# Retention outputs of the first key tile in three single passes, with weights and values split into a rounded part and a remainder

## The reference, cut to what matters

```python
scores = jnp.einsum('bhncd,bhnsd->bhncs', qf, kf) * decay[None, :, None]
o_intra = jnp.einsum('bhncs,bhnse->bhnce', scores, vf)
```

## Time and profile before

| | |
|---|---|
| median of 3 runs | 1299.32 us (1299.04 to 1299.36) |
| the profiled execution | 1299.08 us, its span 1297.3 us |
| PE busy | 1275.5 us, 98% |
| DVE busy | 881.3 us, 68% |
| ACT busy | 684.4 us, 53% |
| POOL busy | 49.4 us, 4% |
| chain that ended last | PE 97%, DVE 1%, ACT 1% |
| mean granted TensorE clock | 0.997 |

### The profile page before, as it was taken

The page is one execution under the profiler, slowest core; times in us unless marked ns, Lnnn a source line. Parts: engine busy times, 40 slices in busy tenths (PEclk is TensorE's granted clock), DMA queues, the critical chain, the costliest instruction groups (busy, mean ns, idle before and its releaser), DMA issues.

```text
span 1297.3 us, 26115 instructions
## 1 busy us (share of the span) xinstructions
PE 1275.5 (98%) x10282; PEld 1270.3 (98%) x10282; DVE 881.3 (68%) x1098; ACT 684.4 (53%) x894; POOL 49.4 (4%) x47
## 2 busy tenths in 40 slices
PE   6999999999999999999999999999999999999996
PEld 6999999999999999999999999999999999999996
DVE  7666555877775786665566665568788777766654
ACT  5444445757766554444454444457578565544531
POOL 1000001000000010000010000010000001000000
PEclk9999999999999999999999999999999999999998
DMA  7555555544334555555545555545543444655551
GB/s 273 190 171 175 177 172 172 178 163 147 131 129 134 174 168 179 179 176 178 179 163 182 175 178 178 178 165 179 172 137 131 147 160 165 208 183 193 172 193 59
DMA packets 61217, 219.30 MB, mean 169 GB/s; under 512 B 6992, under 2 KB 8144, under 8 KB 61008
## 3 DMA queue, kind: packets, MB, share of 16 engines
q1 hardware_dynamic: 60704, 217.53, 50.3%
q10 hardware_dynamic: 432, 0.59, 0.1%
HBM read 217.04 MB, written 1.05 MB: 168 GB/s over the span
## 4 chain that ended last, share of the span: by engine, by line
PE 97%; DVE 1%; ACT 1%; DMA 0%; issue 0%; DVEq 0%; ACTq 0%
PE bank L984 31%; PE bank L983 31%; PE bank L985 31%; PE bank L1105 1%; PE bank L1196 1%; PE bank L1225 1%; PE bank L1094 1%; DVE w_lo L611 0%; PE bank L1077 0%; DMA gain<-gains 0%; DVE xg L619 0%; PE bank L1112 0%; PE bank L997 0%; PE bank L1237 0%; PE bank L1095 0%; ACT xh L396 0%
## 5 line engine op out<-in xcount | busy, mean ns | idle before, releaser
L611 DVE TENSOR_TENSOR w_lo<-raw,w_hi 128x1024 fp32r<-128x1024 f32 x408 | 511.1, 1259 | 258.5 <-ACT w_hi L390 252.6
L983 PE MATMUL bank<-xh,w_hi 128*128 128x272 f32 (+1 forms) x2240 | 644.1, 288 | 11.9 <-DVE xl L625 11.4
L984 PE MATMUL bank<-xl,w_hi 128*128 128x272 f32 (+1 forms) x2240 | 642.2, 287 | 0.0
L985 PE MATMUL bank<-xh,w_lo 128*128 128x272 f32 (+1 forms) x2240 | 640.3, 286 | 0.0
L390 ACT ACTIVATE w_hi<-raw 128x1024 fp32r<-128x1024 f32 x408 | 428.7, 1057 | 398.4 <-PE bank L985 393.2
L983 PEld LDWEIGHTS bank<-xh,w_hi 128*128 128x128 f32 x2240 | 423.3, 189 | 12.9 <-DVE xl L625 10.3
L984 PEld LDWEIGHTS bank<-xl,w_hi 128*128 128x128 f32 x2240 | 421.7, 188 | 0.2
L985 PEld LDWEIGHTS bank<-xh,w_lo 128*128 128x128 f32 x2240 | 421.8, 188 | 0.0
L983 PE MATMUL bank<-gh,w_hi 128*128 128x272 f32 (+1 forms) x1024 | 292.9, 286 | 0.0
L984 PE MATMUL bank<-gl,w_hi 128*128 128x272 f32 (+1 forms) x1024 | 292.1, 285 | 0.0
L985 PE MATMUL bank<-gh,w_lo 128*128 128x272 f32 (+1 forms) x1024 | 291.9, 285 | 0.0
(11 more groups left out here) (170 smaller groups left out, 700.7 us busy)
## 6 DMA issues: line engine op xcount, KB each, us to landing
raw<-stream SPq DMA_DIRECT2D x408, 512.0 KB, 3.3
table<-tables SPq DMA_DIRECT2D x1, 1424.0 KB, 8.0
out<-h SPq DMA_DIRECT2D x4, 256.0 KB, 2.4
h<-tokens ACTq DMA_DIRECT2D x2, 272.0 KB, 5.8
h<-tokens SPq DMA_DIRECT2D x2, 272.0 KB, 5.8
rv_gb<-squares SPq DMA_DIRECT2D x1, 384.0 KB, 8.4
square<-squares SPq DMA_DIRECT2D x1, 128.0 KB, 7.9
gain<-gains ACTq DMA_DIRECT2D x1, 28.0 KB, 5.2
```

What stands on the lines that cost most here:

```text
L611: eng.tensor_tensor(w_lo[:, slot, :], raw[:, slot, :], w_hi[:, slot, :].bitcast(F32), ALU.subtract).then_inc(lo_ready, 1)
L983: pe.matmul(out, wh, hi, start=first, stop=False)
L984: pe.matmul(out, wh, lo, start=False, stop=False)
L985: mm = pe.matmul(out, wl, hi, start=False, stop=last)
```

## The change: what it does

The output of the first key tile is no longer a float32 matmul of `rv` and `dec`. Both are split into a rounded part and a remainder of the type float32r, and three single-pass matmuls take its place: rounded values by rounded weights, rounded values by the weights' remainder, the values' remainder by rounded weights. The product of both remainders is left out. The second key tile stays a float32 matmul.

- ACT writes `dec_hi` in each even step, after the logarithm and exponential of the head before; it waits for the first step of `ret_decayed`, and for PE's output of the head before.
- DVE writes `dec_lo` right after its two decay instructions; it waits for `dec_rounded`.
- PE's output waits for `dec_split` in place of `ret_decayed`.
- The values are split once per layer: four copies of 256 columns on ACT in steps 11, 13, 15, 17, and eight subtractions of 128 columns on DVE in steps 19, 21, 22, 23, into free chunks of `gh` and `gl`.

```diff
+RV_HI, RV_LO = [11, 13, 15, 17], [19, 21, 22, 23]
+        dec_hi = sb("dec_hi", [P, T], F32R)
+        dec_lo = sb("dec_lo", [P, T], F32R)
@@ ACT, in the mixer's step s
+                    if s in RV_HI:
+                        k = RV_HI.index(s)
+                        eng.wait_ge(v_ready, l * 6 + k + 1)
+                        eng.activation(rv_hi(2 * k, 2), rv[:, 0, 2 * k * DV:(2 * k + 2) * DV], ACT.Copy).then_inc(rv_rounded, 1)
...
+                    hd = (s - RET0) // 2
+                    if (s - RET0) % 2 == 0 and 0 <= hd < HEADS:
+                        if hd:
+                            eng.wait_ge(ret_o, l * HEADS + hd)
+                        eng.wait_ge(ret_decayed, l * 2 * HEADS + 2 * hd + 1)
+                        eng.activation(dec_hi[:, qf:T], dec[:, qf:T], ACT.Copy).then_inc(dec_rounded, 1)
@@ DVE, in the mixer's step s
+                    if s in RV_LO:
+                        k = RV_LO.index(s)
+                        eng.wait_ge(rv_rounded, l * 4 + k + 1)
+                        for hd in (2 * k, 2 * k + 1):
+                            eng.tensor_tensor(rv_lo(hd), rv[:, 0, hd * DV:(hd + 1) * DV], rv_hi(hd).bitcast(F32),
+                                              ALU.subtract).then_inc(rv_split, 1)
...
                         eng.tensor_tensor(dec[:, T:SCORES], bank[:, 4, T:SCORES], table[:, c:c + T - P], ALU.mult).then_inc(ret_decayed, 1)
+                        eng.wait_ge(dec_rounded, l * HEADS + hd + 1)
+                        eng.tensor_tensor(dec_lo[:, qf:T], dec[:, qf:T], dec_hi[:, qf:T].bitcast(F32), ALU.subtract).then_inc(dec_split, 1)
@@ PE, in the mixer's step s
-                        pe.wait_ge(ret_decayed, l * 2 * HEADS + 2 * (hd + 1))
+                        pe.wait_ge(dec_split, l * HEADS + hd + 1)
+                        if hd == 0:
+                            pe.wait_ge(rv_split, l * HEADS + HEADS)
...
-                        for i, (t0, _) in enumerate(TILES):
-                            q = max(t0, qf)
-                            c = SEG[i] + q - t0
-                            mm = pe.matmul(bank[:, 5, q:T], rv[:, i, hd * DV:(hd + 1) * DV],
-                                           dec[:, c:c + T - q], start=(i == 0), stop=(i == 1))
-                        mm.then_inc(ret_o, 1)
+                        pe.matmul(bank[:, 5, qf:T], rv_hi(hd), dec_hi[:, qf:T], start=True, stop=False)
+                        pe.matmul(bank[:, 5, qf:T], rv_hi(hd), dec_lo[:, qf:T], start=False, stop=False)
+                        pe.matmul(bank[:, 5, qf:T], rv_lo(hd), dec_hi[:, qf:T], start=False, stop=False)
+                        pe.matmul(bank[:, 5, P:T], rv[:, 1, hd * DV:(hd + 1) * DV], dec[:, T:SCORES], start=False, stop=True).then_inc(ret_o, 1)
```

More of the change, by code:

```diff
@@ L190, in all_pairs, with rv_hi, rv_lo @@
             return x[:, :].rearrange("p (c t) -> p c t", t=T)
+        def rv_hi(hd, n=1):
+            return (gh if hd < 4 else gl)[:, FC - 4 + hd % 4 // 2, hd % 2 * DV:(hd % 2 + n) * DV]
+        def rv_lo(hd):
+            g, c = (gh if hd < 3 or hd == 6 else gl), (hd % 3 * DV if hd < 6 else SCORES)
+            return g[:, FC - 2:FC, :].rearrange("p a t -> p (a t)")[:, c:c + DV]
         def stack_chunk(branch, hd):
@@ L279, in trunk @@
         rq_tail_in, sq_tail_in = sem("rq_tail_in"), sem("sq_tail_in")
+        rv_rounded, rv_split, dec_rounded, dec_split = sem("rv_rounded"), sem("rv_split"), sem("dec_rounded"), sem("dec_split")
         y_merged, yh_ready, y_ready = sem("y_merged"), sem("yh_ready"), sem("y_ready")
```

## The result

The changed kernel takes 1304.90 us (median of 5 runs, 1304.73 to 1305.17), the kernel before 1299.32. The ratio is 1.0045 with an interval of 1.0033 to 1.0056: slower by 5.6 us. The forecast was 1303.5.

A forecast was written before the change was run, and what follows sets the result against it. PE's stream bounds the kernel, together with any result PE waits for that comes later. Terms 3.7 + 0.5 + 1.0 less 0.95 saving give +4.3 us on 1299.1; with 0.24 for the median, 1303.5, range 1299.5 to 1307.5.

The forecast's parts named there:

- The saving: PE's first-key-tile output in three single passes: 0.083 us less per head in layer 0, about 0.073 in layer 1, 1.25 together.
- The first term: Outputs of heads 0 to 3 and 5 late behind the split weights: 1.84 us in layer 0, 1.88 in layer 1, 3.7 together.
- The relay: DVE's first product, ACT's rounding, DVE's remainder, then PE: 1.52 us from the product's start in layer 0, 1.47 in layer 1.
- The second and third term: Work queued behind DVE's and ACT's waits: head 5's variance late, 0.5 us; start of stick-breaking late, 1.0 us.
- layer 1 repeats the pattern with 256 columns: Layer 1's outputs of heads 0 to 3 and 5 late by 0.51, 0.27, 0.53, 0.10 and 0.47 us, 1.88 in sum.
- rival 1: PE's stream absorbs the lateness and only the saving is left, 1298.1 us; half-hidden 1300 to 1301.5; chance 0.24 with both forms.
- rival 2: Pushed-back work cascades: w_lo and evictions become late, each of 16 heads costs some 0.7 more than its saving, 1310 us; chance 0.15.
- That the change would be faster: Third rival: the whole kernel gains more than 0.2%, below 1296.7 us; chance 0.03.

The follow-up runs named there:

- work only: The changed kernel with all added ACT and DVE work, but PE computes the float32 product and waits only for the decay products: 1303.69 us against 1299.24, ratio 1.0034.

## Why the prediction was right, and where its sizes were off

**The saving** was 1.25 us and is 1.05 to 1.20, by the kernel with three passes alone.

**The first term** (outputs late) held in place and sign. In layer 0 the forecast was 0.55, 0.30, 0.57, 0.13 and 0.29 for heads 0 to 3 and 5; the lags, with the saving of 0.08 put back, give 0.57, 0.39, 0.19, 0.20 and 0.30. Heads 4, 6 and 7 don't wait. Head 2 is low because head 1's variance is late before it, by 0.44. Heads 1 and 2 together, this variance included, were forecast at 0.87 and lost 1.03. The relay was taken as 1.35 to the remainder's end and measures 1.38 in head 0 and 1.43 in most others: there the product's end and ACT's start lie 0.10 us apart and not 0.03. Only heads behind the first have ACT's second wait (`ret_o`) in front of the rounding; that it is the cause wasn't tried.

**The second and third term** held in layer 0: head 5's variance and the start of stick-breaking, from step 36 to 42, were forecast at 0.25 + 0.53 and lost 0.78. The size is partly luck. The forecast had a single wait at the start of stick-breaking, and that one (L1126) lost 0.42. Another 0.21 went in step 37, where I had nothing: stick-breaking's first scores start 0.10 us late behind ACT's copies, and the tail's cumulated sums 0.09. Layer 0 as a whole: 2.1 forecast, 2.49 measured.

**The step that was mis-sized** is "layer 1 repeats the pattern with 256 columns". It was given 2.2 us and lost 3.1. Up to step 36 it lost 1.78 where I had 1.44 (the outputs less the saving). Head 4's variance loses 0.44 us where I had 0, but head 5's output behind it then only 0.04 where I had 0.40, so that the pair is near. The larger part is between steps 36 and 42, 1.34 where I had 0.73: head 5's variance 0.37, step 37 with the copies and the tail's sums 0.36, head 7's output 0.16, and the second stick-breaking split 0.41. From step 32 on, a piece has 24 matmuls at 0.117 or 0.118 instead of 0.125 us, and step 33 as a whole takes PE 3.44 us in layer 1 and 3.65 in layer 0, while DVE's and ACT's instructions shrink by 0.02 each. From the end of the split of the square to the start of the variance, head 4 had 0.49 us in layer 0 and 0.31 in layer 1, head 5 0.44 and 0.26, both in the kernel before. For the outputs I had read layer 1's own rows. For the variances and the start of stick-breaking I took layer 0's steps over with the shorter relay, and not the shorter piece.

**A step that failed without showing in the sum** is that there were separate terms. I priced what is queued behind the relay at 0.5 + 1.0 us, counted beside 3.7 for the outputs. Alone it costs 4.4 (work only), and the outputs' wait adds 1.9 to it. A delay in the loop scores, product, output, square, variance, scores is paid once, wherever in it PE meets it first. The sum came out near since I had already taken head 1's variance off head 2's output.

**The rivals.** The hidden relay (rival 1) is excluded by the waits for the remainder, and by the kernel that rounds twice: each 0.46 us more costs 0.43 per head. The cascade (rival 2) did not come: w_lo is no new releaser in the mixers, and DVE's idle time ahead of w_lo at head 1 is 2.44 us, against 2.20 before. That the change would be faster was excluded by its own saving of 1.1 us.

**What stays open.** Of the 5.8 us, 0.22 are lost after the mixer, at the start of layer 1's second feed-forward, where PE waits once for w_lo. It shows in six of the eleven changed kernels and not in the others. The six are those in which ACT rounds the decayed scores, except the one that rounds twice, and their lags before it run from 0.22 to 6.27 us; I didn't find its cause.

## What to carry to other kernels

When PE is 98% busy, the price of an edit is not in the busy shares but in the distance between each helper's result and the matmul that needs it; list that distance head by head before adding a hand-over. A relay over two engines costs both engines their place in the queue, not only its own length, so price what stands behind each wait, and count a loop once. Before moving an instruction forward, ask what its engine will do while it waits: idle time that is free outside the loop costs inside it.

## What the runs showed of the hardware that I had not expected

DVE doesn't take up its own result at once: with a semaphore between two of its instructions, 0.10 us of idle time lay between L961's end (295.44) and L964's start (295.54) in the kernel where DVE rounds, where instructions without a wait overlap by 0.08. How long it stands differs: in the changed kernel, L774 ends at 303.69 and L777, which reads its result, starts at 303.73. A copy of 128 x 272 and its hand-over that is added to such a relay costs about 0.43 us of PE's time, nearly the copy's own length, though PE's busy share stays at 98% in all eleven kernels.
